# Second halves of one expert's gate and up weights issued behind the last merge, and one of them kept in another buffer

## The reference

```python
def _merge(outs, gate_logits, w_branch, w_out):
    g = jax.nn.sigmoid(gate_logits.astype(jnp.float32)).astype(gate_logits.dtype)
    g = g.reshape(*g.shape[:-1], N_BRANCHES, D_MODEL)
    y = g[..., 0, :] * (outs[0] @ w_branch[0])
    for n in range(1, N_BRANCHES):
        y = y + g[..., n, :] * (outs[n] @ w_branch[n])
    return y @ w_out

def _moe(h, w_router, router_bias, w_gate, w_up, w_down):
    ...
    combine = _route(hf, w_router, router_bias).astype(h.dtype)
    for e in range(N_EXPERTS):
        a = jax.nn.silu(hf @ w_gate[e]) * (hf @ w_up[e])
        y = y + combine[:, e:e + 1] * (a @ w_down[e])

...
        x = x + g1 * _merge((o_a, o_b, o_n), gate_l, w_branch[l], w_out[l])
...
        x = x + g2 * _moe(_modulate(x, norm2[l], sh2, sc2), w_router, router_bias,
                          w_e_gate[l], w_e_up[l], w_e_down[l])
```

## Time and profile before

| | us |
|---|---|
| median of three runs | 1568.55 |
| lowest, highest | 1566.22, 1569.42 |
| the profiled execution | 1573.06 |
| its span, first to last instruction | 1571.4 |

### The profile page before, as it was taken

How to read it: one execution, slowest core, us unless ns; L and a number is a source line. 1 busy time by engine, 2 the same in 40 slices (tenths; PEclk the granted TensorE clock), 3 DMA queues, 4 the chain that set the end, 5 groups by cost and what they waited for, 6 DMA issues and landing times. The chain is left out here.

```text
span 1571.4 us, 19180 instructions
## 1 busy us (share of the span) xinstructions
PE 1508.7 (96%) x7346; PEld 850.9 (54%) x7346; DVE 743.1 (47%) x1554; ACT 377.7 (24%) x908; POOL 144.7 (9%) x233
## 2 busy tenths in 40 slices
PE   8999999999999999999999989999999999989897
PEld 4478766666676646644433334456677655333332
DVE  2366278789995435511111245306788837111113
ACT  3022288811111111101111123106821111000001
POOL 0100001200000100001021220000300011111110
PEclk9999999999999998999999999999999997999899
DMA  9823230125744472589999996342149867999996
GB/s 332 275 54 108 73 132 5 38 77 140 273 154 167 157 308 100 188 300 376 391 417 420 393 343 203 137 175 90 42 115 369 314 249 278 384 406 412 409 376 284
DMA packets 110187, 371.89 MB, mean 237 GB/s; under 512 B 25616, under 2 KB 29856, under 8 KB 93540
## 3 DMA queue, kind: packets, MB, share of 16 engines
q1 hardware_dynamic: 96688, 332.42, 57.0%
q0 software_dynamic: 12976, 37.95, 6.8%
q10 hardware_dynamic: 432, 0.29, 0.1%
HBM read 363.20 MB, written 19.73 MB: 244 GB/s over the span
## 5 line engine op out<-in xcount | busy, mean ns | idle before, releaser
L2946 PE MATMUL bank<-ring_sb,HT_sb 128*64 128x512 f32 x544 | 122.9, 605 | 1.8 <-DMA ring_sb<-w_e_up 1.1
L2543 PE MATMUL bank<-ring_sb,HT_sb 128*128 128x512 f32 x256 | 114.9, 605 | 2.5 <-ACT HT_sb L1146 2.5
L1541 DVE SCALAR_TENSOR_TENSOR MB_sb<-ring_sb,cT_sb,MB_sb 128x512 f32<-128x512 f32 x144 | 108.2, 752 | 5.1
L2983 PE MATMUL bank<-ring_sb,QR_sb 128*64 128x512 f32 x336 | 80.9, 625 | 16.6 <-DMA ring_sb<-w_e_down 14.1
L2229 DVE TENSOR_TENSOR QR_sb<-QR_sb,bank 64x512 f32<-64x512 f32 x21 | 21.9, 1045 | 139.8 <-ACT QR_sb L1431 139.8
L2652 PE MATMUL bank<-QR_sb,ring_sb 128*128 128x512 f32 x192 | 86.3, 592 | 0.0
L2543 PEld LDWEIGHTS bank<-ring_sb,HT_sb 128*128 128x128 f32 x256 | 48.9, 194 | 63.1 <-issue 63.1
L2946 PEld LDWEIGHTS bank<-ring_sb,HT_sb 128*64 128x64 f32 x544 | 39.1, 139 | 74.2 <-issue 73.0
L2666 PEld LDWEIGHTS bank<-tab_sb,MB_sb 128*128 128x128 f32 x480 | 51.3, 141 | 44.6 <-issue 41.6
L2695 PE MATMUL bank<-KR_sb,QR_sb 64*128 64x512 f32 (+1 forms) x288 | 70.5, 568 | 3.9 <-ACT MB_sb L1348 2.9
L2666 PE MATMUL bank<-tab_sb,MB_sb 128*128 128x128 f32 x480 | 68.5, 280 | 1.7 <-DVE MB_sb L1880 1.4
(11 more groups left out here) (459 smaller groups left out, 2571.4 us busy)
## 6 DMA issues: line engine op xcount, KB each, us to landing
ring_sb<-w_e_down SPq DMA_DIRECT2D x32, 2048.0 KB, 18.3
ring_sb<-w_mod SPq DMA_DIRECT2D x24, 2048.0 KB, 9.9
ring_sb<-w_in SPq DMA_DIRECT2D x21, 2048.0 KB, 13.5
ring_sb<-w_e_gate SPq DMA_DIRECT2D x16, 2048.0 KB, 13.0
ring_sb<-w_e_up SPq DMA_DIRECT2D x16, 2048.0 KB, 17.2
ring_sb<-w_e_gate SPq DMA_DIRECT2D x22, 1024.0 KB, 16.5
ring_sb<-w_e_up SPq DMA_DIRECT2D x22, 1024.0 KB, 18.7
ring_sb<-w_branch SPq DMA_DIRECT2D x8, 1024.0 KB, 12.0
```

What stands on the lines that cost most here:

```text
L1541: link(stt(a, WR[slot][:, k], cT[:, k, strm:strm + 1], a, ALU.mult, ALU.add))
L2543: ins = mm(bank[j % 4][:, :], HT[:, k, P * t:P * t + P], WR[slot][:, k], start=(k == 0), stop=(k == KD - 1))
L2946: ins = mm(bank[0][HALF * side:HALF * side + HALF, :], hgT[q % 2][:, k, 0:HALF], w[k], start=(k == 0), stop=(k == KD - 1))
L2983: ins = mm(bank[4][HALF * half:HALF * half + HALF, :], eaT[:, k, 0:HALF], w[k][:, CW * half:CW * half + CW], start=(k == 0), stop=(k == 3))
```

## The change

In the second layer, the second halves of the third expert's gate and up weights are issued right after its first halves, ahead of the down matrices of the first two experts, instead of behind them. Both wait for the last merge instead of for the last square root and the last router product. So that this is allowed, the second half of up goes to `QR[2D:4D]` instead of the upper half of `HT` (for the later experts in the same place too), and in the second layer ScalarE's squares are written to `KR[0:2D]` instead of `WK`.

```diff
-            (KR[:, 2 * D:4 * D], HT[:, KD // 2:KD].rearrange("p a b -> p (a b)")))]
+            (KR[:, 2 * D:4 * D], QR[:, 2 * D:4 * D]))]
...
                 if q == 2 and half:
-                    eng.wait_ge(*((router_mm, 2 * L) if j else (rms_done, NT * 3 + NLAT)))
+                    eng.wait_ge(merged, before(merge_jobs, L))
...
                 for q in range(2):
                     load_pair(l, q, q)
                 if l:
-                    for j in range(2):
-                        load_half(2, 2, j, 0)
+                    for half in range(2):
+                        for j in range(2):
+                            load_half(2, 2, j, half)
                 load_expert(l, 0, 0, 2)
                 if l:
                     load_expert(l, 1, 1, 2)
-                    for j in range(2):
-                        load_half(2, 2, j, 1)
                 eng.wait_ge(order_ready, l + 1)
...
-                    norm_root(t, junk[1])
+                    norm_root(t, [KR[:, D * i:D * i + D] for i in range(NLAT)] if l else junk[1])
```

## The result

| | before | changed |
|---|---|---|
| median, us | 1569.76 | 1574.82 |
| lowest to highest of six | 1566.22 to 1571.33 | 1573.38 to 1575.47 |
| span of the profiled execution | 1571.4 | 1573.7 |

The ratio is 1.0031, with a 95% interval from 1.0016 to 1.0046: the changed kernel is about 5 us slower. The two profiled executions can't be compared by their spans as they stand. The stretch ahead of the last merge, which the change doesn't touch, took 2.76 us less in this execution (the merge ends at 1265.78 + 0.69 = 1266.47 here and at 1269.23 in the earlier trace rows). From there to the end of the span the changed kernel takes 307.2 us (1573.7 - 1266.47) and the kernel before 302.2 (1571.4 - 1269.23), 5.1 us less, as in the medians.

The account below looks back on a forecast made before the run. It took the experts as bound by weight traffic, started by a dependency chain through VectorE's wait for MB. 2.2 us (MB's landing) plus 0.8 (clock) made 3.0, from 1568.55 to 1571.5 us; range 1566.5 to 1575.0.

Parts of the forecast that it names:

- clearly slower, by the clock: Rival: TensorE's slow stretch lasts through the first expert's products, 4.7 us more, 7.7 us in all, 1576.2 us; chance 0.15.
- within 0.2%: Outcome for the whole kernel's time: no more than 0.2% from the kernel before; chance 0.51.
- slower: Outcome for the whole kernel's time: slower by more than 0.2%; chance 0.42.
- Queue order and the new wait: SP's queue: second halves issue right after the first halves, near 1271.1 and 1271.6; the wait is already met, 1.8 us spare.
- Gain 0 from the early landing: Third expert's second halves and the down matrices: landing sooner gains 0; the halves were already hidden by some 27 us.
- MB late by 2.2 us, between 0.8 and 2.5: POOL's scale and shift rows, sharing DMA engines with SP's longer queue, land 2.2 us later, delaying VectorE; bounds 0.8 to 2.5.
- The tail behind the bulk: DMA's first burst: the last engine's share of POOL's rows lands 1.7 us after the bulk ends.
- The clock, 0.8 us, between 0 and 1.33: TensorE: the first tile's router products fall into the 1.2 GHz stretch, costing 0.8 us; 1.33 if wholly, 0 if not.
- The rest moves rigidly: From VectorE's second residual through router, routing and fourth expert's loads to the DMA-bound rest, everything moves by 2.2 us.
- Hidden both ways: Rival: scale and shift rows on POOL's queue are not late, so the time stays 1568.5 us; chance 0.15.
- Faster, by the clock: Rival: TensorE's slow stretch over the first expert's gathering and products, 4.5 us, disappears; sum -2.3 us, 1566.2 us; chance 0.10.

Follow-up runs that it names:

- e2_behind_rows: The changed kernel, with the two second halves also waiting until POOL's rows of scale and shift have landed; 1.0003 to the kernel before.
- e9_fill_again: The changed kernel with six products nobody reads in TensorE's hole ahead of the second tile's transposes, run a second time; 1.0007 to the kernel before.
- e3_one_half: The changed kernel, with only gate's second half issued early and up's put behind the down matrices; 1.0030 to the kernel before.
- e1_place: The changed kernel with SP's old load order put back, keeping the new places in QR and KR; 0.9997 to the kernel before.
- e6_pool_more: The kernel before, with POOL loading two more unread rows (1 MB) ahead of scale and shift; 1.0034 to the kernel before.
- e8_after_again: The changed kernel measured once more, on one chip with the filled kernels; 1.0029 to the kernel before.
- e5_latent_before: The kernel before, with POOL loading only the latent stream's output gate, scale and shift rows in the second layer; 0.9995 to the kernel before.

## Why the prediction came out as it did

The time, 1574.82, lies just inside the range, 3.3 us above the forecast; 1.2 of these are the kernel before, which measured 1569.76 and not 1568.55 this time. The direction and the mechanism were right; the size was not: 5.1 us in the medians where 3.0 were worked out. The forecast's own bounds, 0.8 to 3.8 us, don't hold that. The range reached up to 1575.0 only because it took in most of the rival "clearly slower, by the clock", which did not come about, so that the time lies inside it is partly luck. The chances put a little more on "within 0.2%" than on "slower", and it was the latter.

- *Queue order and the new wait*: right. The halves go out at M+1.9 without a pause.
- *Gain 0 from the early landing*: right. With the collision removed, e2_behind_rows measures 1.0003.
- *MB late by 2.2 us, between 0.8 and 2.5*: 2.50 in the changed kernel, 2.4 to 2.6 in the other traces with the collision but one (2.95 in e9_fill_again). The tail behind the bulk stayed as it was (1.9 us from about 1292.0 to 1293.90, where the prediction read 1.7), so the upper bound would have been the better choice. The share of a third by turns was right, and e3_one_half confirms it in the point where it differs from a count of bytes. The Trainium skill's arbitration rule (DMA: Bandwidth & Descriptors, Queues, rings and completion order) is that each engine goes round the queues that have work, a packet at a time. The trace agrees: 693 packets of SP and 688 of POOL in 18 us.
- *The clock, 0.8 us, between 0 and 1.33*: this is the term that was mis-sized. From MB's landing to the logits it takes 13.53 us instead of 11.53, 2.0 us more. Three pieces make it up: the first tile's router products 3.21 against 1.86 (1.35), the transposes between the two batches at half clock (1.09 against 0.63: 0.46), and the second batch 3.43 against 3.19 (0.24). The step counted the first piece alone, and only partly. That the fall would come "as early or earlier" was near enough: M+33.8 against M+33.5. The size varies between executions: from MB's landing to the logits it takes 10.68 to 12.25 us in the three traces with MB on time (before, e1_place, e2_behind_rows) and 13.53 to 14.16 in the four with MB late and no filling (changed, e3_one_half, e6_pool_more, e8_after_again).
- *The rest moves rigidly*: right in the mean. Logits +4.50, fourth expert's load +4.47 (M+63.24 against 58.77), second expert +4.47; the remaining half microsecond is within what single executions differ by. But the fourth expert's load was the wrong start to go by. In e5_latent_before (last merge until 1266.16) it is issued at M+53.19, 5.6 us sooner than before, and the time is 0.9995. What stays is the issue of the fifth expert's first load, right behind the second expert's products: M+70.81 there, M+70.97 in the kernel before, M+75.45 in the changed kernel. There both loads were late by 4.5 us, so the sum did not feel it. Timelines of SP, fourth and fifth expert's first loads in e5_latent_before, then the fifth's in the kernel before:

```profile
1319.35 0.35 SPq L788 DMA_DIRECT2D ring_sb<-w_e_gate  x1
1336.97 0.34 SPq L788 DMA_DIRECT2D ring_sb<-w_e_gate  x1
...
1340.20 0.34 SPq L788 DMA_DIRECT2D ring_sb<-w_e_gate  x1
```

- *Hidden both ways*: fell with MB's landing. *Clearly slower, by the clock*: its stretch was the same as before, 6.63 + 8.75 us against 5.90 + 9.52.
- *Faster, by the clock*: its price of 4.5 us was wrong, and the experiments show why. In e1_place and e5_latent_before the gathering and the first expert's products ran at the upper level, and neither was faster. The reason is VectorE: from the logits to its first product of the first expert it takes 24.1 to 24.3 us in every trace (table), a list of small instructions that no clock of TensorE changes. In e1_place TensorE then stood waiting for it, and the second expert's products ran partly at the lower level in their turn (8.37 us instead of 7.09):

```profile
1320.23 3.79 PE L2874 MATMUL bank<-MB_sb,QR_sb 128*128 128x64 f32 x32
1327.39 0.68 PE L2859 MATMUL bank<-tab_sb,QR_sb 64*128 64x64 f32 x4 [3.37 <-DVE QR_sb L2229]
1328.00 1.11 PE L3018 MATMUL bank<-tab_sb,MB_sb 128*128 128x128 f32 x4
1329.04 8.37 PE L2946 MATMUL bank<-ring_sb,HT_sb 128*64 128x512 f32 x32
```

So behind the logits, TensorE's slow stretch lies beside VectorE's routing and was nearly hidden; ahead of the logits it is on the path. The prediction treated both as on the path.

## What to carry to other kernels

Before a bulk load is issued earlier, look at which small load of another queue is in flight at that time and who waits for it: here one megabyte that nobody needed for 80 us delayed rows that VectorE was already waiting for. Keep it behind that load with a wait, or shrink the small load, and expect no gain from the earlier issue where the reader never waited. Where a delay moves small products into a slow stretch of TensorE's clock, price all that then lies in it, transposes too, unless longer work of another engine runs beside it. And before a load is taken for the start of a stretch that is bound by weight traffic, look at what the next loads wait for.

## What the runs showed of the hardware that was not expected

- Two queues shared the DMA engines by turns (693 and 688 packets in 18 us), and the cost of an added load levelled off: 1.05 MB (e3_one_half) and 2.1 MB both delayed the other queue's last rows, by 2.6 and 2.5 us. Smaller loads were not tried.
- The granted clock fell at M+33.5 in the kernel before, where TensorE had stood idle for 0.48 us, and at M+33.8 in the changed kernel, after 2.96 us; in the other three runs with MB late and no filling at M+32.7 to M+33.0. With four or six products of 512 columns (1.88 or 2.74 us) in the gap it fell at M+37.0 to M+37.6, and the first sixteen router products took 1.86 us in each of these three traces. It is not the same in every execution: in e2_behind_rows, with MB on time, it stayed at the upper level until M+42.7.
